# A hybrid diffusion trunk on one core: the beginning of the kernel rebuilt around un-modulated pooling

## The chip, the cores and the metric

The kernel runs on one core of one Trainium2 chip, as one program. The metric is device time in microseconds (us) of one execution; lower is better. The engines are named as in the profile: PE (TensorE, matrix products), DVE (VectorE), ACT (ScalarE), POOL (GpSimd) and SP (SyncE, which here only issues transfers). PEld is PE's loading of weights.

## The reference

The reference is one inference step of four layers over 128 context tokens and 256 latent tokens of width 1024. Each layer has a token mixer and a convolutional feed-forward block (FFN), and each of these eight sub-layers is modulated by vectors taken from a conditioning vector. What the change touches is the very first sub-layer, the pooling mixer of layer 0, and the modulation vectors that it needs:

```python
def modulation(cond, w, b):                      # six vectors of 1024 for each layer
    m = jax.nn.silu(cond) @ w + b
    return m.reshape(m.shape[:-1] + (N_MOD, D_MODEL))
def modulate_in(x, mod, k, g):
    return rms_norm(x, g) * (1.0 + mod[:, None, 3 * k + 1]) + mod[:, None, 3 * k]
def gated_residual(x, out, mod, k, g):
    return x + mod[:, None, 3 * k + 2] * rms_norm(out, g)
def pool_mixer(h, w, scale):
    ...
        mean = (csg[:, hi] - csg[:, lo]) / (hi - lo).astype(jnp.float32)[None, :, None]
        outs.append(mean - hf[..., sl])          # for each of four window lengths, 256 channels each
    p = jnp.stack(outs, axis=2).astype(h.dtype)
    y = jnp.einsum('blgc,gcd->blgd', p, w).reshape(h.shape)
    return y * scale
```

## The kernel before

All five engines run instruction lists written out by hand and meet at semaphores; each engine executes its own list strictly in order, and so does SP, which issues nearly all transfers. So a transfer that waits on SP holds back all transfers behind it.

**Pieces.** The modulation vectors are products of a two-column conditioning vector with `w_mod`. One vector of 1024 takes four pieces of 1024 KB (`MOD_PIECES = 4`); `load_mod(p)` loads piece p, `mod_piece(p)` multiplies it on PE (8 small matmuls; the trace counts 16) and then frees its buffer through the semaphore `mod_used`. Before the first FFN, 32 pieces pass: 20 for the first five vectors (SCALE0, SHIFT0, GATE0, SCALE1, SHIFT1) in seven buffers (`START_SLOTS = 7`, piece p in buffer p mod 7, so that load p waits until PE has used p-7), then 12 for the next three vectors in nine buffers. Below they are called p0 to p31. DVE's `mod_vector(i)` transposes a finished vector out of PSUM, and `coefficient` multiplies in the norm gains.

**The beginning.** PE's list (`pool_mix`) multiplies p0 to p7; turns the first scale and shift into rows, which ACT copies (`copy_row`) and stores to DRAM; SP reads them back broadcast over all partitions (`row0`, two transfers of 1024 KB). PE multiplies p8 to p11. DVE makes the modulated rows `h_rows` from x, the inverse norm and the two broadcast rows. Then PE pools: for each of eight blocks k of 128 channels, one matmul of 129 columns and two of 257 against `pool_m`, into bank 6 or 7 in turn; ACT rounds the result to `h_hi`, DVE makes the remainder `h_lo` and frees the bank (`pooled_lo`). Then p12 to p19, then the pooling mixer's weights (72 matmuls), then the gated residual of the three token chunks, between which p20 to p31 are multiplied and the three chunks are turned for the FFN (`turn_unit`). The FFN's first matmul (line 1693) needs all three turned chunks, and in PE's list the third turn stands behind p31.

**The gate.** The residual needs the gate vector GATE0 as a broadcast row: PE turns it (`turn_gate(0)`), ACT stores it, SP loads it as `gb` (`load_gate(0)`); DVE's `weigh` waits for it.

Of the kernel before, what the change touches and what calls it, by code (L numbers as in the profile page):

```python
# [14 lines left out]
P = 128  # L15
D = 1024
# [134 lines left out]
def build_trunk(nc, a, out):  # L151
# [4 lines left out]
    with ExitStack() as ctx:  # L156
# [50 lines left out]
        with ExitStack() as part:  # L207
            pool_m = sb("pool_m", [P, len(WINDOWS), POOL_W], F32, part)
            row0 = sb("row0", [P, 2, 2, D], F32, part)
            h_rows = sb("h_rows", [P, 3, D], F32, part)  # L210
            mod_more = sb("mod_more", [P, START_SLOTS - 2, 2 * D], F32, part)
# [5 lines left out]
        with ExitStack() as part:  # L217
            sb("mod_row0_under", [P, len(WINDOWS), POOL_W], F32, part)
            mod_row0 = sb("mod_row0", [P, 2, 2 * D], F32, part)
# [46 lines left out]
        rows_dram = nc.dram_tensor("rows_dram", [2 + 2 * DEPTH, 16 * P], F32, kind="Internal").ap()  # L266
# [14 lines left out]
        log_dt = flat_wk[:, 704:896]  # L281
        x_end = by_dir(flat_wk[:, 1536:2048])
# [18 lines left out]
        def mod_bank(i):  # L301
            if i < START_VECTORS:
                return bank(3 if i % 2 else 5)[:, 0:MOD_BANK_COLS]
# [25 lines left out]
        row0_loaded = sem("row0_loaded")  # L329
# [105 lines left out]
        LOADS0 = 16 * 9  # L435
# [98 lines left out]
        def _(sp):  # L534
# [19 lines left out]
            def load_gate(t):  # L554
                if t:
                    sp.wait_ge(weighed, event(t, 0))
                sp.wait_ge(row_stored[t % 2], 16 * (t // 2 + 2))
                sp.dma_start(gb[:, :, :].rearrange("p s n -> p (s n)"),
                             rows_dram[2 + t:3 + t, :].broadcast_to([P, 2 * D])).then_inc(gb_loaded, 16)
# [26 lines left out]

# [238 lines left out]
        def _(act):  # L825
# [60 lines left out]

            def transition(t, n):
# [25 lines left out]
            def ffn_in(l):  # L913
                s = lin[f"ffn_in{l}"]
                p0 = l * PAIRS
                for j in range(FFN_TILES):
# [7 lines left out]
                    if j == 3:  # L924
                        copy_row(2 + 2 * l + 1)
# [7 lines left out]
            def ssd_conv():  # L933
                s = lin["ssd_conv"]
                for j in range(CONV_TILES):
# [3 lines left out]
                    if j == 3:  # L939
                        copy_row(4)  # L940
# [68 lines left out]
            def conf_mix():  # L1009
# [17 lines left out]
                for m in range(2 * KD):  # L1027
# [10 lines left out]
                    if m == 3:  # L1038
                        copy_row(6)
# [32 lines left out]
            def qk_mix():  # L1072
                s = lin["qk"]
                for i in range(QK + 1):
                    if i < QK:
# [6 lines left out]
                        if i == 3:  # L1082
                            copy_row(8)
# [49 lines left out]
            copy_row(1)  # L1133
            round_to(2)
            copy_row(2)
            for k in range(KD):
                act.wait_ge(pooled, k + 1)
                act.activation(h_hi[:, k, :], bank(6 + k % 2)[:, 0:COLS], ACT.Copy).then_inc(pooled_hi, 1)
            transition(0, lin["ffn_in0"].n0)
# [34 lines left out]
        def _(vec):  # L1174
# [54 lines left out]
            def weigh(t, c):  # L1229
# [7 lines left out]
                if t in (0, 4):  # L1237
                    if t == 4:
# [1018 lines left out]
```

## Time and profile before

| | us |
|---|---|
| median of 3 runs (2098.22 to 2098.79) | 2098.58 |
| the profiled execution, its own time | 2101.43 |
| its span in the trace | 2099.7 |
| first matmul of the first FFN in the trace | 128.39 |
| PE busy in the span | 1970.1 (94%) |

The profiled execution took 2.85 us more than the median, of which 1.73 us lie outside its span. The busy share is one over the whole span; the beginning, which is the only part that the change edits, looks quite different and is read from its own rows.

### The profile page before, as it was taken

The page shows a single profiled execution, that of the slowest core. Times are in us where ns is not written, and L with a number is a line of the kernel's source. Part 1 is how long each engine was busy: PE and PEld are TensorE (multiplying, and loading weights), DVE is VectorE, ACT ScalarE, POOL GpSimd, SP SyncE. Part 2 cuts the span into 40 slices and gives each one's busy share as a digit, 9 for nine tenths or more (in the row PEclk, how much of TensorE's full clock was granted, in tenths as well). Part 3 has the DMA queues.
Part 4 walks back from the last instruction along what each step waited for, and adds up shares of the span by engine and source line. Part 5 has one row for each costly group of instructions (what it writes and reads, how often), then busy time and mean ns, then how long its engine had stood idle before and what let it go on. Part 6 is the DMA issues. An engine that isn't in the chain of part 4 may idle for free.

```text
span 2099.7 us, 30072 instructions
## 1 busy us (share of the span) xinstructions
PE 1970.1 (94%) x11801; PEld 1744.9 (83%) x11801; DVE 1195.5 (57%) x1773; ACT 919.6 (44%) x1552; POOL 701.1 (33%) x515
## 2 busy tenths in 40 slices
PE   3779999999999989999999998899999969899998
PEld 1469998799998877799987865799987857799986
DVE  0567772366534565777733853777723674777722
ACT  1244442444545554544423424544424434544422
POOL 0033324233334445332243741323242321332342
PEclk6889999999999999999999999999999979999999
DMA  9954346544330135543454674444364413244442
GB/s 366 372 222 150 122 120 220 179 134 130 116 126 20 34 121 224 213 148 121 127 205 171 223 196 180 182 145 127 121 215 179 180 46 111 77 144 122 129 123 78
DMA packets 80667, 326.41 MB, mean 155 GB/s; under 512 B 9072, under 2 KB 17808, under 8 KB 66704
## 3 DMA queue, kind: packets, MB, share of 16 engines
q1 hardware_dynamic: 78928, 322.57, 44.5%
q8 instruction: 94, 1.54, 0.3%
q10 hardware_dynamic: 1600, 1.93, 0.3%
q14 instruction: 45, 0.37, 0.1%
HBM read 319.34 MB, written 5.12 MB: 155 GB/s over the span
## 4 chain that ended last, share of the span: by engine, by line
PE 82%; DVE 6%; ACT 4%; DMA 3%; issue 2%; POOL 1%; SPq 1%; DVEq 0%; ACTq 0%; POOLq 0%
PE pair L1693 17%; PE pair L1695 17%; PE pair L1694 17%; PE pair L1727 7%; PE pair L1728 6%; PE pair L1729 6%; PE pair L1841 3%; DMA mod_more<-in_w_mod 2%; DVE x L1253 2%; PE pair L1935 1%; ACT junk L863 1%; PE pair L1881 1%; PE pair L1846 1%; DMA ssd_cols<-in_ssd_cols 1%; DVE wk L1244 1%
## 5 line engine op out<-in xcount | busy, mean ns | idle before, releaser
L712 POOL TENSOR_TENSOR w_lo<-raw,w_hi 128x512 fp32r<-128x512 f32 (+1 forms) x375 | 574.7, 1534 | 1150.9 <-ACT w_hi L835 1150.7
L1693 PE MATMUL pair<-h_hi,w_hi 128*128 128x386 f32 (+1 forms) x2008 | 689.4, 343 | 18.8 <-POOL h_lo L719 16.2
L1695 PE MATMUL pair<-h_hi,w_lo 128*128 128x386 f32 (+1 forms) x2008 | 684.7, 341 | 0.0
L1694 PE MATMUL pair<-h_lo,w_hi 128*128 128x386 f32 (+1 forms) x2008 | 683.9, 341 | 0.0
L1186 DVE TENSOR_TENSOR w_lo<-raw,w_hi 128x512 fp32r<-128x512 f32 x351 | 430.6, 1230 | 317.1 <-ACT w_hi L835 317.0
L835 ACT ACTIVATE w_hi<-raw 128x1024 fp32r<-128x1024 f32 x375 | 392.8, 1050 | 285.3 <-PE pair L1729 224.5
L1693 PEld LDWEIGHTS pair<-h_hi,w_hi 128*128 128x128 f32 (+1 forms) x2008 | 381.8, 190 | 24.4 <-POOL h_lo L719 22.1
L1694 PEld LDWEIGHTS pair<-h_lo,w_hi 128*128 128x128 f32 (+1 forms) x2008 | 382.6, 191 | 0.9
L1695 PEld LDWEIGHTS pair<-h_hi,w_lo 128*128 128x128 f32 (+1 forms) x2008 | 381.7, 190 | 0.3
L1310 DVE SCALAR_TENSOR_TENSOR acc<-pair,taps,acc 128x385 f32<-128x385 f32 x176 | 108.8, 618 | 214.8 <-ACT acc L922 214.8
L922 ACT ACTIVATE acc<-pair,taps 128x386 f32<-128x386 f32 x176 | 117.4, 667 | 238.3 <-PE pair L1695 238.3
L1728 PE MATMUL pair<-w_hi,g 128*128 128x512 f32 x528 | 208.5, 395 | 0.0
L1729 PE MATMUL pair<-w_lo,g 128*128 128x512 f32 x528 | 208.4, 395 | 0.0
L1727 PE MATMUL pair<-w_hi,g 128*128 128x512 f32 x528 | 208.3, 395 | 0.0
L1727 PEld LDWEIGHTS pair<-w_hi,g 128*128 128x128 f32 x528 | 99.2, 188 | 23.4
L1728 PEld LDWEIGHTS pair<-w_hi,g 128*128 128x128 f32 x528 | 99.3, 188 | 23.3
L1729 PEld LDWEIGHTS pair<-w_lo,g 128*128 128x128 f32 x528 | 99.2, 188 | 23.3
L920 ACT ACTIVATE g<-gate 128x386 fp32r<-128x386 f32 x84 | 44.3, 527 | 162.4 <-DVE gate L1323 162.4
L1317 DVE SCALAR_TENSOR_TENSOR acc<-pair,taps,acc 128x385 f32<-128x385 f32 x176 | 108.5, 616 | 3.2
L991 ACT ACTIVATE mod_raw<-pair,shift 128x128 f32<-128x128 f32 x192 | 53.8, 375 | 32.0 <-PE pair L1846 31.9
L719 POOL TENSOR_TENSOR h_lo<-stage,h_hi 128x512 fp32r<-128x512 f32 x21 | 32.0, 1522 | 92.4 <-ACT h_hi L885 92.4
L1448 DVE TENSOR_TENSOR mod_raw<-mod_raw,pair 128x512 f32<-128x512 f32 x48 | 32.3, 685 | 53.3 <-ACT mod_raw L991 53.3
(277 smaller groups left out, 2195.6 us busy)
## 6 DMA issues: line engine op xcount, KB each, us to landing
raw<-in_ffn_in SPq DMA_DIRECT2D x176, 512.0 KB, 3.5
raw<-in_ffn_out SPq DMA_DIRECT2D x88, 512.0 KB, 3.6
mod_raw<-in_w_mod SPq DMA_DIRECT2D x32, 1024.0 KB, 7.5
mod_base<-in_w_mod SPq DMA_DIRECT2D x31, 1024.0 KB, 7.4
mod_more<-in_w_mod SPq DMA_DIRECT2D x20, 1024.0 KB, 13.7
raw<-in_ssd_conv SPq DMA_DIRECT2D x32, 512.0 KB, 3.5
gb<-rows_dram SPq DMA_DIRECT2D x8, 1024.0 KB, 5.2
raw<-in_ssd_z SPq DMA_DIRECT2D x16, 512.0 KB, 3.4
```

The source lines that it names most:

```text
L712: pool.tensor_tensor(w_lo[:, m % SLOTS, 0:w], raw[:, m % SLOTS, 0:w], w_hi[:, m % SLOTS, 0:w].bitcast(F32), ALU.subtract).then_inc(w_low_p ...
L835: act.activation(w_hi[:, m % SLOTS, 0:w], raw[:, m % SLOTS, 0:w], ACT.Copy).then_inc(w_rounded, 1)
L922: act.activation(acc[:, j % 4, :], tile_bank(j)[:, 0:COLS], ACT.Identity, scale=taps[:, l, j, 1:2], bias=taps[:, l, j, 3:4]).then_inc(acc_ ...
L1186: vec.tensor_tensor(w_lo[:, m % SLOTS, w0:w1], raw[:, m % SLOTS, w0:w1], w_hi[:, m % SLOTS, w0:w1].bitcast(F32), ALU.subtract).then_inc(w_ ...
L1310: vec.scalar_tensor_tensor(out=acc[:, j % 4, 1:COLS], in0=b[:, 0:COLS - 1], scalar=taps[:, l, j, 0:1], in1=acc[:, j % 4, 1:COLS], op0=ALU. ...
L1317: vec.scalar_tensor_tensor(out=acc[:, j % 4, 0:COLS - 1], in0=b[:, 1:COLS], scalar=taps[:, l, j, 2:3], in1=acc[:, j % 4, 0:COLS - 1], op0= ...
L1693: ten.matmul(to, wh, h_hi[:, k, cols], start=k == 0, stop=False, skip_group_check=True)
L1694: ten.matmul(to, wh, h_lo[:, k, cols], start=False, stop=False, skip_group_check=True)
L1695: ins = ten.matmul(to, wl, h_hi[:, k, cols], start=False, stop=k == KD - 1, skip_group_check=True)
L1727: ten.matmul(to, hi[:, k, cols], wh, start=first, stop=False)
L1728: ten.matmul(to, lo[:, k, cols], wh, start=False, stop=False)
L1729: ins = ten.matmul(to, hi[:, k, cols], wl, start=False, stop=last)
```

## The change

Before, the rows were normalized, scaled and shifted (by broadcast rows) and then pooled. Now the rows are only normalized and then pooled; since pooling is linear along tokens and the scale and shift are per channel, the scale is applied to the pooled block by ACT (`pooled_scaled`) and the shift, times the column sums of the pool matrix, is added by DVE (`pooled_shifted`). The column sums come from 12 matmuls of `pool_m` with a matrix of ones. The two rows through DRAM are gone. PE's own loop over the eight blocks is unchanged, and with it its wait, from block k = 2 on, for the remainder of block k-2 (`pooled_lo`, k-1). The order of transfers, of the pieces on PE, and of the work in the first transition is new.

```diff
@@ SP: order of transfers
-            for p in range(START_SLOTS):
+            for p in range(MOD_PIECES):
                 load_mod(p)
...
+            for p in range(MOD_PIECES, START_SLOTS):
+                load_mod(p)
             sp.dma_start(pool_m[:, :, :], a["pool_m"]).then_inc(loaded0, 16)
...
+            load_mod(START_SLOTS)
+            load_to(2)
+            for p in range(START_SLOTS + 1, 3 * MOD_PIECES):
                 load_mod(p)
-            for r in range(2):
-                sp.wait_ge(row_stored[r], 16)
-                sp.dma_start(row0[:, r, :, :].rearrange("p s n -> p (s n)"),
-                             rows_dram[r:r + 1, :].broadcast_to([P, 2 * D])).then_inc(row0_loaded, 16)
-            for p in range(10, 16):
+            sp.dma_start(rowc[:, :], a["pool_scale"].broadcast_to([P, D])).then_inc(pool_scale_loaded, 16)
+            for p in range(3 * MOD_PIECES, 3 * MOD_PIECES + START_SLOTS):
                 load_mod(p)
-            load_to(2)
             load_gate(0)
-            for p in range(16, MOD_PIECES * START_VECTORS):
+            for p in range(3 * MOD_PIECES + START_SLOTS, MOD_PIECES * START_VECTORS):
                 load_mod(p)
             load_to(4)
+            for to, name in ((taps, "taps"), (ssd_taps, "ssd_taps"), (dt_rows, "dt_rows"), (ssd_cols, "ssd_cols")):
+                sp.dma_start(to[tuple(slice(None) for _ in to.shape)], a[name]).then_inc(tables_loaded, 16)
@@ ACT: scale, then round
+            for k in range(KD + 1):
+                if k < KD:
+                    act.wait_ge(pooled, k + 1)
+                    if k >= 2:
+                        act.wait_ge(pooled_lo, k - 1)
+                    for s, cols in enumerate((slice(0, LAT0), slice(LAT0, COLS))):
+                        ins = act.activation(pooled_v[k % 2][:, cols], bank(6 + k % 2)[:, cols], ACT.Identity,
+                                             scale=coef[:, 0, 0, s, k:k + 1])
+                    ins.then_inc(pooled_scaled, 1)
+                if k:
+                    act.wait_ge(pooled_shifted, k)
+                    act.activation(h_hi[:, k - 1, :], pooled_v[(k - 1) % 2], ACT.Copy).then_inc(pooled_hi, 1)
@@ DVE: shift, then remainder
+            for k in range(KD + 1):
+                if k < KD:
+                    vec.wait_ge(pooled_scaled, k + 1)
+                    v = pooled_v[k % 2]
+                    for s, cols in enumerate((slice(0, LAT0), slice(LAT0, COLS))):
+                        ins = vec.scalar_tensor_tensor(out=v[:, cols], in0=pool_sums[:, k // 2, cols],
+                                                       scalar=modc[:, 0, SHIFT0, s, k:k + 1], in1=v[:, cols],
+                                                       op0=ALU.mult, op1=ALU.add)
...
+                if k:
+                    vec.wait_ge(pooled_hi, k)
+                    vec.tensor_tensor(h_lo[:, k - 1, :], pooled_v[(k - 1) % 2], h_hi[:, k - 1, :].bitcast(F32),
+                                      ALU.subtract).then_inc(pooled_lo, 1)
@@ PE: pool_mix
-                for p in range(2 * MOD_PIECES):
+                for p in range(MOD_PIECES):
                     mod_piece(p)
...
+                ten.wait_ge(loaded0, LOADS0)
+                for g in range(len(WINDOWS)):
+                    to = bank((0, 1, 2, 4)[g])
+                    ten.matmul(to[:, 0:LAT0], ones[:, :], pool_m[:, g, 0:LAT0], start=True, stop=True, skip_group_check=True)
...
-                for p in range(3 * MOD_PIECES, START_VECTORS * MOD_PIECES):
+                for p in range(2 * MOD_PIECES, 3 * MOD_PIECES):
                     mod_piece(p)
+                turn_gate(0)
...
-                fill(0, 0, 3)
+                ten.wait_ge(weighed, event(0, 0) + 1)
+                for p in range(3 * MOD_PIECES, 4 * MOD_PIECES):
+                    mod_piece(p)
                 turn_unit(0, 0)
-                fill(0, 3, 7)
+                for p in range(4 * MOD_PIECES, START_VECTORS * MOD_PIECES):
+                    mod_piece(p)
+                ten.wait_ge(mod_read, START_VECTORS)
+                fill(0, 0, 7)
                 turn_unit(0, 1)
                 fill(0, 7, None)
                 turn_unit(0, 2)
```

SP's list, from the transfers behind `pool_m` to the first FFN weights. `mod_raw` and `mod_more` are pieces, `raw` weights, `rowc` the pooling scale, `gb` the gate row; the brackets name the semaphores that an issue waits for. Before:

```order
L542 DMA mod_raw<-in_w_mod 128x2048 [waits mod_used] x2
L542 DMA mod_more<-in_w_mod 128x2048 [waits mod_used]
L577 DMA row<-rows_dram 128x2048 [waits row_stored0]
L577 DMA row<-rows_dram 128x2048 [waits row_stored1]
L542 DMA mod_more<-in_w_mod 128x2048 [waits mod_used] x4
L542 DMA mod_raw<-in_w_mod 128x2048 [waits mod_used] x2
L551 DMA raw<-in_pool 128x1024 x2
L558 DMA gb<-rows_dram 128x2048 [waits row_stored0]
L542 DMA mod_more<-in_w_mod 128x2048 [waits mod_used] x4
L551 DMA raw<-in_ffn_in 128x1024 x2
```

Now:

```order
L545 DMA mod_raw<-in_w_mod 128x2048 [waits mod_used]
L554 DMA raw<-in_pool 128x1024 x2
L545 DMA mod_raw<-in_w_mod 128x2048 [waits mod_used]
L545 DMA mod_more<-in_w_mod 128x2048 [waits mod_used] x3
L577 DMA rowc<-in_pool_scale 128x1024
L545 DMA mod_more<-in_w_mod 128x2048 [waits mod_used] x2
L545 DMA mod_raw<-in_w_mod 128x2048 [waits mod_used] x2
L545 DMA mod_more<-in_w_mod 128x2048 [waits mod_used] x3
L561 DMA gb<-rows_dram 128x2048 [waits row_stored0]
L545 DMA mod_more<-in_w_mod 128x2048 [waits mod_used]
L554 DMA raw<-in_ffn_in 128x1024 x2
```

The two row transfers are gone, and the gate row moved from behind p15 to behind p18.

PE's list around the pooling loop, of which the first and the last block stand here. Lines 1664 and 1711 are the pieces (8 matmuls each), 2093 to 2097 and 2131 to 2148 products with `pool_m`, 2116 and 2169 the first of the mixer's weights. Before:

```order
L1664 MATMUL pair<-mod_raw,cond 32x256 x8
L1664 MATMUL pair<-mod_more,cond 32x256 x24
L1672 MATMUL pair<-ident,coef 16x128
L2093 MATMUL pair<-pool_m,h_rows 128x129
L2097 MATMUL pair<-pool_m,h_rows 128x257 x2
...
L1664 MATMUL pair<-mod_more,cond 32x256 x16
L1664 MATMUL pair<-mod_raw,cond 32x256 x16
L1664 MATMUL pair<-mod_more,cond 32x256 x32
L2116 MATMUL pair<-w_hi,h_hi 128x256
```

Now:

```order
L2131 MATMUL pair<-pool_m,ones 128x129
L2134 MATMUL pair<-pool_m,ones 128x257 x2
L1711 MATMUL pair<-mod_more,cond 32x256 x24
L1711 MATMUL pair<-mod_raw,cond 32x256 x8
L2144 MATMUL pair<-pool_m,h_rows 128x129
L2148 MATMUL pair<-pool_m,h_rows 128x257 x2
...
L1711 MATMUL pair<-mod_raw,cond 32x256 x8
L1711 MATMUL pair<-mod_more,cond 32x256 x24
L1719 MATMUL pair<-ident,coef 16x128
L2169 MATMUL pair<-w_hi,h_hi 128x256
```

The sums and p4 to p7 now stand ahead of the loop, p8 to p11 moved from ahead of it to behind it, and p12 to p19 left this stretch for one further down, behind the mixer's weights.

DVE's list in the pooling loop, from its second block on. Before, `L1618 TENSOR_TENSOR h_lo<-pair,h_hi` stood eight times in a row; now:

```order
L1656 SCALAR_TENSOR_TENSOR stage<-wk,modc,stage 128x129 [waits pooled_scaled]
L1656 SCALAR_TENSOR_TENSOR stage<-wk,modc,stage 128x257
L1665 TENSOR_TENSOR h_lo<-stage,h_hi 128x386 [waits pooled_hi]
L1656 SCALAR_TENSOR_TENSOR stage<-wk,modc,stage 128x129 [waits pooled_scaled]
L1656 SCALAR_TENSOR_TENSOR stage<-wk,modc,stage 128x257
L1665 TENSOR_TENSOR h_lo<-stage,h_hi 128x386 [waits pooled_hi]
```

The remainder of block k now stands behind the shift of block k+1.

## Rows read from the trace of the kernel before

**Rows 1.** Page: chain that ended last, share of the span by engine.

```profile
PE 82%; DVE 6%; ACT 4%; DMA 3%; issue 2%; POOL 1%; SPq 1%; DVEq 0%; ACTq 0%; POOLq 0%
```

**Rows 2.** Chain that ended last, 0 to 220 us: start us, us, what.

```profile
96.67 23.20 DMA mod_more<-in_w_mod
119.92 1.93 PE pair L1664 x16
128.39 0.66 PE pair L1693
```

**Rows 3.** Timeline, 0 to 40 us: start, us, operation, [idle <-releaser].

```profile
6.26 1.94 PE L1664 MATMUL pair<-mod_raw,cond 128*32 128x256 f32 x16 [6.26 <-DMA mod_raw<-in_w_mod]
21.10 1.94 PE L1664 MATMUL pair<-mod_more,cond 128*32 128x256 f32 x16 [0.55 <-DMA mod_more<-in_w_mod]
32.89 1.06 ACT L1130 ACTIVATE junk<-x 128x1024 bf16<-128x1024 f32 x1 [30.04 <-DMA ssd_cols<-in_ssd_cols]
```

**Rows 4.** Stretches: engines' busy time (x instructions), PEclk, DMA share, GB/s.

```profile
37.00:42.00 5.00, 3.73 (x38) 1.56 (x34) 1.03 (x5) 1.78 (x6) 0.00 (x0) 0.50 0.35 107
63.00:69.00 6.00, 5.99 (x17) 4.59 (x18) 2.88 (x4) 3.25 (x5) 3.45 (x2) 0.53 0.29 95
77.00:83.00 6.00, 4.95 (x92) 2.50 (x80) 0.80 (x3) 0.00 (x0) 0.00 (x0) 1.00 0.84 313
```

**Rows 5.** SP's own waits, 0 to 135 us: total us, times, longest.

```profile
SPq L558 <- DMA rows_dram<-grow: 22.2, 1, 22.2
```

**Rows 6.** Timeline of the pooling loop, 62 to 78 us.

```profile
62.84 0.80 PE L2093 MATMUL pair<-pool_m,h_rows 128*128 128x129 f32 x2 [6.98 <-DVE h_rows L1614]
63.43 1.92 PE L2097 MATMUL pair<-pool_m,h_rows 128*128 128x257 f32 x4
65.14 0.64 PE L2093 MATMUL pair<-pool_m,h_rows 128*128 128x129 f32 x2
70.60 0.49 PE L2093 MATMUL pair<-pool_m,h_rows 128*128 128x129 f32 x2
70.93 1.03 PE L2097 MATMUL pair<-pool_m,h_rows 128*128 128x257 f32 x4
72.00 0.49 ACT L1138 ACTIVATE h_hi<-pair 128x386 fp32r<-128x386 f32 x1 [0.95 <-PE pair L2097]
72.52 0.56 DVE L1618 TENSOR_TENSOR h_lo<-pair,h_hi 128x386 fp32r<-128x386 f32 x1 [0.88 <-ACT h_hi L1138]
73.14 0.49 PE L2093 MATMUL pair<-pool_m,h_rows 128*128 128x129 f32 x2
75.52 1.93 PE L1664 MATMUL pair<-mod_more,cond 128*32 128x256 f32 x32
```

**Rows 7.** Timeline of the first transition, 110 to 114 us.

```profile
111.46 1.36 DVE L1271 TENSOR_SCALAR stage<-pair,coef,modc 128x128 f32<-128x128 f32 x4
112.35 1.49 ACT L876 ACTIVATE stage<-pair,modc,coef 128x128 f32<-128x128 f32 x4
```

**Rows 8.** Groups by line and shape, whole run: busy us, mean ns.

```profile
L922 ACT ACTIVATE acc<-pair,taps 128x386 f32<-128x386 f32 x176 | 117.4, 667 | 238.3 <-PE pair L1695 238.3
L1310 DVE SCALAR_TENSOR_TENSOR acc<-pair,taps,acc 128x385 f32<-128x385 f32 x176 | 108.8, 618 | 214.8 <-ACT acc L922 214.8
```

**Rows 9.** DMA issues, 0 to 135 us: KB each, us from issue to landing.

```profile
gb<-rows_dram SPq DMA_DIRECT2D x1, 1024.0 KB, 4.5
```

**Rows 10.** Timeline of the first gated residual, 86 to 92 us.

```profile
88.26 1.22 DVE L1240 TENSOR_TENSOR wk<-pair,rowc 128x1024 f32<-128x1024 f32 x1 [2.35 <-PE pair L2118]
90.77 1.23 DVE L1244 TENSOR_TENSOR wk<-wk,gb 128x1024 f32<-128x1024 f32 x1 [1.29 <-ACT junk L847]
```

**Rows 11.** Stretches around two changes of the granted clock (columns as rows 4).

```profile
68.00:69.00 1.00, 1.00 (x5) 0.88 (x5) 0.56 (x1) 0.02 (x1) 0.11 (x1) 0.66 0.75 164
97.00:102.00 5.00, 2.70 (x38) 1.22 (x36) 3.68 (x5) 3.86 (x9) 1.27 (x1) 1.00 1.01 419
102.00:103.00 1.00, 0.59 (x12) 0.39 (x16) 1.00 (x4) 1.00 (x2) 0.00 (x0) 0.91 1.06 442
```

More of the change, by code:

```diff
@@ L281, in build_trunk @@
         log_dt = flat_wk[:, 704:896]
+        pool_sums = flat_wk[:, 0:len(WINDOWS) * COLS].rearrange("p (g n) -> p g n", g=len(WINDOWS))
+        pooled_v = [flat_stage[:, k * 512:k * 512 + COLS] for k in range(2)]
         x_end = by_dir(flat_wk[:, 1536:2048])
@@ L302, in mod_bank @@
             if i < START_VECTORS:
[L303 removed]
+                return bank((5, 3, 5, 0, 1)[i])[:, 0:MOD_BANK_COLS]
             r = (i - START_VECTORS) % END_VECTORS
@@ L885, in unit_high, with transition0 @@
                 act.activation(h_hi[:, :, cols], stage[:, e % 2, :, :], ACT.Copy).then_inc(h_hi_ready, 1)
+            def transition0(n):
+                for c in range(3):
+                    first(0, c)
+                    second(0, c)
+                round_to(n + 2)
+                for c in range(3):
+                    unit_stage(0, c)
+                    unit_high(0, c)
+                act.wait_ge(tables_loaded, 64)
+                round_to(n + 4)
             def transition(t, n):
@@ L1131, in _ @@
                 root(c)
-            copy_row(0)
[L1133 to L1139, printed above, removed]
+            act.wait_ge(coef_ready, 1)
+            for k in range(KD + 1):
[10 more added lines that the diff above has]
+                    act.activation(h_hi[:, k - 1, :], pooled_v[(k - 1) % 2], ACT.Copy).then_inc(pooled_hi, 1)
+            round_to(2)
+            copy_row(0)
+            transition0(lin["ffn_in0"].n0)
             for l in range(DEPTH):
@@ L1280, in unit_low, with transition0 @@
                                   ALU.subtract).then_inc(h_lo_dve, 1)
+            def transition0(n):
+                for c in range(2):
+                    weigh(0, c)
+                    residual(0, c)
+                    unit(0, c)
+                mod_vector(3)
+                coefficient(0, 2)
+                weigh(0, 2)
+                residual(0, 2)
+                low_to(n + 2)
+                mod_vector(4)
+                vec.wait_ge(mod_done, START_VECTORS)
+                unit_stage(0, 0)
+                unit(0, 2)
+                unit_low(0, 0)
+                for c in (1, 2):
+                    unit_stage(0, c)
+                    unit_low(0, c)
+                vec.wait_ge(tables_loaded, 64)
+                low_to(n + 4)
+                end_vectors(0)
             def transition(t, n):
@@ L1601, in _ @@
             vec.wait_ge(consts, CONSTS)
+            for c in range(3):
+                invert(c)
+                vec.tensor_scalar(h_rows[:, c, :], x[:, c, :], inv[:, c:c + 1], None, ALU.mult).then_inc(rows_ready, 1)
+            vec.wait_ge(sums_made, 1)
+            for g in range(len(WINDOWS)):
+                ch.did(vec.tensor_copy(pool_sums[:, g, :], bank((0, 1, 2, 4)[g])[:, 0:COLS]))
             mod_vector(0)
@@ L2078, in pool_mix @@
             def pool_mix():
-                for p in range(2 * MOD_PIECES):
+                for p in range(MOD_PIECES):
                     mod_piece(p)
-                ten.wait_ge(coef_ready, 1)
-                turn_row(0, coef[:, 0, 0, :, :].rearrange("p s k -> p (s k)"))
-                ten.wait_ge(mod_done, 2)
-                turn_row(1, modc[:, 0, SHIFT0, :, :].rearrange("p s k -> p (s k)"))
-                for p in range(2 * MOD_PIECES, 3 * MOD_PIECES):
+                ten.wait_ge(loaded0, LOADS0)
+                for g in range(len(WINDOWS)):
+                    to = bank((0, 1, 2, 4)[g])
+                    ten.matmul(to[:, 0:LAT0], ones[:, :], pool_m[:, g, 0:LAT0], start=True, stop=True, skip_group_check=True)
+                    for c in (1, 2):
+                        at = LAT0 + (c - 1) * (LAT + 1)
+                        ins = ten.matmul(to[:, LAT0:COLS], ones[:, :], pool_m[:, g, at:at + LAT + 1],
+                                         start=c == 1, stop=c == 2, skip_group_check=True)
+                ins.then_inc(sums_made, 1)
+                for p in range(MOD_PIECES, 2 * MOD_PIECES):
                     mod_piece(p)
-                turn_gate(0)
                 ten.wait_ge(rows_ready, 3)
```

74 lines of the change are left out of this document (29 added, 45 removed).

## The prediction

> **What bounds the kernel now.** The page comes first: PE is busy 94% of the span (table above) and makes 82% of the chain that ended last [rows 1]. Behind the first FFN matmul the program is the same row for row, and PE is its bound; so the change is worth what it does to the moment of that matmul, 128.39 us. The chain up to there, read next, ends in one load: p31, issued at 96.67, is used by PE at 119.92, and 8.5 us of turning and rounding lie between that and 128.39 [rows 2]. The beginning therefore waits for bytes, and the question is how long the DMA engines need for all that lies up to p31.
>
> The stretches show when they work. In a busy stretch seven pieces start on PE between 6.26 and 21.10, so 1024 KB take 14.84 / 6 = 2.47 us [rows 3]; I call 1024 KB a unit. There are three holes: DMA share 0.35 from 37 to 42, 0.29 from 63 to 69, 0.84 from 77 to 83, idle 3.25 + 4.25 + 1 = 8.5 us [rows 4]. The middle one is a wait on SP: the gate row's issue waited 22.2 us for its stored row [rows 5], what was queued ran out, and nothing behind it could start. The ledger up to p31: 32 pieces, x 1.5 units, `pool_m` 1.26, pooling weights 1, four FFN chunks 2, gate row 1, two `row0` rows 2, scale 0.5, tables and gains 0.65: 41.9 units, 103.5 us; a start of 6.26 - 2.47 = 3.8; about 2 us for six small transfers (from p6 at 21.10 to the first use at 32.89 pass 3.9 units, 9.6 us, in 11.8 [rows 3]); holes 8.5. Sum 117.8, against 119.92.
>
> **The change, as the same ledger.** The two `row0` rows go: 2 units, 4.9 us saved. All else is loaded still. So the change stands or falls by the holes, and a hole opens when SP stands at a piece whose buffer PE has not freed. Two such places are new.
>
> *First hole.* p15 takes the buffer of p8, and p8 now stands behind PE's whole pooling loop. When does that loop end?
> - SP's start: p0 to p3, x, gains, p4 to p6, `pool_m`: 13.65 us for p3, then 5.9 units (14.6) and 0.7 for two small transfers: everything for the rows is there at 28.95, against 32.89 before [rows 3].
> - 12 sum matmuls are four blocks of the pooling loop's shapes. [...] So two blocks at 2.30, one at 1.9, one at 1.36: 36.8. DVE normalizes the rows (three passes) meanwhile, and its four copies of the sums and first two vectors lie beside PE's p4 to p7.
> - p4 to p7: 4 x 0.95 (two pieces in 1.93 [rows 6]): 40.6.
> - Blocks 0 and 1: 2 x 1.36 (70.60 to 71.96 [rows 6]): 43.3.
> - From then on the loop is one chain. PE's block k+1 waits for the remainder of block k-1; on DVE that stands behind the shift of block k; which waits for ACT's scale of block k; which waits for PE's block k. Before, the same wait hung on one round of ACT 0.49 and DVE 0.56 in two banks, PE going on in the other [rows 6]; eight blocks took 62.84 to 75.52, 12.7 us.
> - The pair of ACTIVATEs (129 and 257 columns): no such row exists. Four of 128 columns take 1.49, so the next starts after 0.37 [rows 7]; 386 columns take 0.67 [rows 8]; between them 257 columns are about 0.56. Pair 0.93; no less than one of 386, 0.67. The pair of shifts on DVE likewise from 1.36 / 4 = 0.34 less the overlap, 0.32 [rows 7], and 0.62 for 385 columns [rows 8]: 0.32 + 0.51 = 0.83, at least 0.62. The remainder 0.56, handovers 0.04, 0.03 and 0.06 [rows 6].
> - Length of one round: at the high clock 1.36 + 0.93 + 0.83 + 0.56 + 0.13 = 3.81 us; at the low clock, where a block takes 62.84 to 65.35, 2.51 [rows 6], 4.96.
> - Which clock? PE would work 1.36 of 3.81 us, a share of 0.36. The nearest rows: from 97 to 102 PE worked 2.70 of 5 us at the high clock, and within 102 to 103 the clock fell [rows 11]. So it should fall in the loop as well, after some us: I take block 2 high, 3 to 7 low. First remainder: 43.3 + 0.04 + 0.93 + 0.03 + 0.83 + 0.56 = 45.7; one high round 49.5; four low rounds 69.35; block 7 2.57 later, 71.9; p8 1.93 (low clock, as in [rows 3]), 73.85.
> - A lone transfer of one unit lands 4.5 us after its issue [rows 9]: p15 at 78.45.
>
> Meanwhile the queue is empty: behind `pool_m` come p7 to p14, pooling weights and scale, 9.5 units, done at 28.95 + 23.5 = 52.4 (p11 waits for p4's use, at 37.8, in time). The hole is 78.45 - 2.47 - 52.4 = 23.6 us.
>
> *Second hole.* p16 to p18 and the gate row follow without a gap, 88.35 (its row is stored at about 82: p11 used at 79, then vector, turn, copy and store). p19, next on SP, takes the buffer of p12; PE's p12 now waits for the first weighing, which waits for the gate row. Weighing took 88.26 to 92.0 [rows 10], 3.75; p12 another 1.0; issue to landing 4.6: p19 at 97.7, where 2.47 would do. Hole 6.9 us. SP's queue behind p19 waits with it: FFN chunks, tables, p20 to p31.
>
> *Rest.* From p19: two FFN chunks 1 unit, tables 0.5 unit and 1.4 us for four small transfers, p20 to p28, two chunks, p29 to p31: 14.5 units and 1.4, 37.2 us. p31 at 134.9, 15.0 us later than 119.92. The reordered residuals are costed at nothing, since this DMA time covers them: DVE's three weighings and what now stands between them take some 23 us from 92 on, so PE's new wait for the fifth vector ends at about 115; p20 to p31 (12 x 0.95), one turn and the unchanged 8.5 us make 136. Were the loads sooner, that chain would end the beginning, 7 us below the 134.9 + 8.5 = 143.4 of the loads.
>
> Sum: minus 4.9 for bytes, plus 30.5 of new holes, minus 8.5 of old holes, minus the 2.1 by which the ledger falls short of 119.92: plus 15. On the profiled execution 2101.43 + 15.0 = 2116.4; that execution lies 2.85 above the median shown, so against the median 2098.58 the forecast is **2113.5 us**.
>
> [...]
>
> **Rivals.**
> 1. *The clock stays high through the loop*: five low rounds and block 7 fall to high ones. First remainder 45.7, five rounds of 3.81, block 7, p8 0.97: 67.15, 6.7 earlier: plus 8.3. With the shortest pairs (0.67, 0.62) a round is 3.34, 2.4 less: plus 5.9. For it: from 97 to 102 the clock held for 5 us of half-busy work; against it: it fell right after [rows 11], the loop is less busy than that, and it lasts longer.
> [...]
> 2. *The clock never rises before the loop*: sums 9.4, pieces 7.7, blocks 4.8, all rounds 4.96: p8 at 82.55, 8.7 later: plus 23.7. Against it: dense work from 62.84 raised it within 68 to 69 [rows 6, 11], and sums and pieces are as dense.
> 3. *The loop overlaps as before*, its stages running side by side: 12.7 us from 40.6, p8 at 54.3, 19.6 earlier: minus 4.7, 2094 us. It decides from p8 at 58.9 on, a round of 2.2 us; the three engines' shortest rows in series make 3.34, and the waits make them a series.
> 4. *No change*: holes as large as those removed, p8 at 55 to 63. It needs rounds of 1.5 to 3.0 us; between rivals 1 and 3.
>
> **How the numbers follow.** About 0.2% (4.2 us) is what a measurement of this kernel can tell from none. Forecast (mostly low rounds) 0.47, rival 1 0.27, rival 2 0.14, rival 3 0.05, rival 4 0.07. The range leaves out rivals 3 and 4 and the far end of 2: plus 5.5 to plus 22, 2104 to 2120.5. Slower 0.88, same 0.07, faster 0.05; the first three cases are all slower.
>
> **What would show it.** Right: DMA share near zero from about 53 to 75 and again for 7 us after the gate row's landing; PE's blocks in the pooling loop 3.8 to 5 us apart, each released by DVE's remainder; p15 released on SP by p8; the first FFN matmul near 143. Wrong: blocks under 2.3 us apart, or p15 issued before 55, would put it at 128 or earlier; a first FFN matmul that does not follow p31 by about 8.5 us would mean that another chain has taken over.

## The result, and the profile after

The change made the kernel slower: 2118.25 us (median of 5 runs, 2114.94 to 2118.53) against 2098.79 us (median of 5 runs, 2098.22 to 2105.13), a ratio of 1.0083, 95% interval 1.0071 to 1.0094. The ratio is taken over the runs of the set; the two medians alone would give 1.0093. The forecast was 2113.5 us in 2104 to 2120.5. The profiled execution took 2116.63 us with a span of 2114.9, 15.2 us more than that of before.

The page gives the chain that ended last, share of the span by engine, as [rows 1]:

```profile
PE 82%; DVE 7%; ACT 5%; issue 2%; DMA 2%; POOL 1%; SPq 0%; DVEq 0%; ACTq 0%; POOLq 0%
```

It still names PE first, and nothing in it points at the beginning. The chain up to the first FFN matmul, which answers to [rows 2], says where the time is (start us, us, what):

```profile
75.17 4.79 DMA rows_dram<-grow
79.97 7.18 DMA gb<-rows_dram
113.56 5.03 PE pair L1711 x48
118.61 16.66 DMA mod_more<-in_w_mod
135.32 1.94 PE pair L1711 x16
143.71 0.66 PE pair L1740
```

p31 is used at 135.32 instead of 119.92, and the first FFN matmul starts at 143.71 instead of 128.39: 15.3 us, all of the difference between the two profiled executions. Behind it 1971.2 us pass up to the end of the span; before, 1971.3.

SP's list shows the two places where it stood (start us, us; the first row holds p14, issued at once, and p15, which waited; the last is p19):

```profile
38.94 30.98 SPq L545 DMA_DIRECT2D mod_raw<-in_w_mod  x2
70.89 2.06 SPq L545 DMA_DIRECT2D mod_more<-in_w_mod  x3
79.97 0.33 SPq L561 DMA_DIRECT2D gb<-rows_dram  x1
93.02 0.33 SPq L545 DMA_DIRECT2D mod_more<-in_w_mod  x1
```

The stretches show the holes that this leaves (columns as [rows 4]; the third from the right is the granted clock, the next the DMA share):

```profile
45.00:50.00 5.00, 2.51 (x6) 1.61 (x6) 1.22 (x3) 1.55 (x6) 0.00 (x0) 0.64 1.02 428
50.00:52.00 2.00, 0.62 (x3) 0.62 (x4) 1.22 (x3) 0.48 (x2) 0.00 (x0) 0.50 0.57 242
52.00:70.00 18.00, 11.76 (x47) 6.97 (x50) 5.06 (x13) 5.33 (x14) 0.00 (x0) 0.50 0.01 2
70.00:73.00 3.00, 2.54 (x44) 1.15 (x36) 2.36 (x3) 1.68 (x2) 2.19 (x2) 0.96 0.80 259
73.00:84.00 11.00, 8.96 (x73) 8.65 (x73) 1.44 (x4) 0.27 (x1) 1.27 (x1) 1.00 0.96 378
84.00:86.00 2.00, 0.00 (x0) 0.00 (x0) 0.00 (x0) 0.00 (x0) 0.00 (x0) 1.00 0.39 156
86.00:93.50 7.50, 2.48 (x24) 1.19 (x28) 3.81 (x4) 2.55 (x5) 0.00 (x0) 0.59 0.02 4
93.50:95.00 1.50, 1.50 (x28) 0.80 (x24) 1.06 (x3) 0.34 (x2) 0.00 (x0) 0.79 0.76 87
95.00:135.00 40.00, 21.28 (x280) 10.32 (x272) 16.60 (x29) 12.81 (x24) 6.37 (x4) 0.75 1.01 420
```

Idle share by length: 0.9 + 17.8 + 0.6 = 19.3 us in the first hole, 1.2 + 7.4 + 0.4 = 9.0 us in the second, 28.3 us in all where before had 8.5. From 95 to 135 the engines never ran dry (DMA share 1.01).

The pooling loop, which answers to [rows 6], one round at the high clock and one at the low (granted clock 1.00 from 40 to 46, 0.50 from 47 to 70; timeline):

```profile
43.34 0.49 PE L2144 MATMUL pair<-pool_m,h_rows 128*128 128x129 f32 x2 [2.08 <-DVE h_lo L1665]
46.78 0.80 PE L2144 MATMUL pair<-pool_m,h_rows 128*128 128x129 f32 x2 [2.08 <-DVE h_lo L1665]
47.38 1.92 PE L2148 MATMUL pair<-pool_m,h_rows 128*128 128x257 f32 x4
49.34 0.73 ACT L1148 ACTIVATE stage<-pair,coef 128x129 f32<-128x129 f32 x2 [3.45 <-PE pair L2148]
50.10 0.75 DVE L1656 SCALAR_TENSOR_TENSOR stage<-wk,modc,stage 128x129 f32<-128x129 f32 x2 [3.37 <-ACT stage L1148]
50.77 0.55 DVE L1665 TENSOR_TENSOR h_lo<-stage,h_hi 128x386 fp32r<-128x386 f32 x1
51.38 0.80 PE L2144 MATMUL pair<-pool_m,h_rows 128*128 128x129 f32 x2 [2.08 <-DVE h_lo L1665]
```

These are four stages of three engines in a row, with only ACT's rounding beside them: PE 2.56, ACT 0.76, DVE's shift 0.67 and its remainder 0.61 make the 4.60 us from 46.78 to 51.38. In each round PE waits 2.08 us for DVE's remainder.

### The profile page after: what moved, and what is told of

Its sections match the earlier page's. It is cut to its first block, busy times and chain, and to the rows that moved or that the text cites. A ratio compares the mean times of both kernels' runs of the same rounds, so it can differ in the third digit from the quotient of the medians.

```text
span 2114.9 us, 30146 instructions
## 1 busy us (share of the span) xinstructions
PE 1974.4 (93%) x11823; PEld 1750.6 (83%) x11823; DVE 1197.0 (57%) x1790; ACT 924.8 (44%) x1566; POOL 701.9 (33%) x515
## 4 chain that ended last, share of the span: by engine, by line
PE 82%; DVE 7%; ACT 5%; issue 2%; DMA 2%; POOL 1%; SPq 0%; DVEq 0%; ACTq 0%; POOLq 0%
PE pair L1740 17%; PE pair L1742 17%; PE pair L1741 17%; PE pair L1774 6%; PE pair L1775 6%; PE pair L1776 6%; PE pair L1888 3%; DVE x L1269 2%; PE pair L1982 1%; ACT junk L861 1%; DMA pool_m<-in_pool_m 1%; DVE wk L1260 1%; PE pair L1928 1%; PE pair L1893 1%; DVE w_lo L1203 1%
## 5 line engine op out<-in xcount | busy, mean ns | idle before, releaser
L1774 PEld LDWEIGHTS pair<-w_hi,g 128*128 128x128 f32 x528 | 99.2, 188 | 23.4
L1776 PEld LDWEIGHTS pair<-w_lo,g 128*128 128x128 f32 x528 | 99.2, 188 | 23.4
```

What stands on the lines that cost most here:

```text
L1774: ten.matmul(to, hi[:, k, cols], wh, start=first, stop=False)
L1776: ins = ten.matmul(to, hi[:, k, cols], wl, start=False, stop=last)
```

## The experiments

Three theories were written down before the runs. **H** is the prediction's: what counts is the DMA time lost while SP stands at a transfer that must wait. **B**: the whole cost lies in p15 standing behind p8. **C**: what grew is the serial chain of pooling, gate row and residuals; loads are late only because nobody needs them sooner. Line numbers in the experiments' rows differ by up to some 30 from those above.

The kernel before was run again beside each set, and each ratio is to the runs of its own set (medians 2100.34 us beside runs 1 to 4, 2099.26 beside 5 to 7, 2098.34 beside 8). The last column is the idle time of the DMA engines from 4 us to p31's use, added up over steps of 1 us.

| kernel | median us (runs) | ratio to before, 95% interval | p15 issued | p19 issued | p31 on PE | first FFN matmul | DMA idle up to p31 |
|---|---|---|---|---|---|---|---|
| before | 2098.79 (5) | 1 | 43.8 | 76.7 | 119.92 | 128.39 | 10.6 |
| changed | 2118.25 (5) | 1.0083 (1.0071 to 1.0094) | 69.6 | 93.0 | 135.32 | 143.71 | 30.3 |
| 1: p8 ahead | 2119.04 (4) | 1.0091 (1.0076 to 1.0107) | 39.5 | 93.7 | 135.93 | 142.82 | 32.2 |
| 2: first hole filled | 2109.13 (4) | 1.0049 (1.003 to 1.0068) | 69.2 | 92.8 | 128.52 | 135.41 | 23.4 |
| 3: second hole filled | 2105.90 (6) | 1.0032 (1.002 to 1.0045) | 70.8 | 94.6 | 128.99 | 135.88 | 23.4 |
| 4: bank wait | 2099.38 (10) | 0.9995 (0.9986 to 1.0004) | 52.0 | 74.4 | 116.62 | 125.11 | 12.9 |
| 5: runs 3 and 4 together | 2090.44 (6) | 0.9952 (0.994 to 0.9964) | 53.5 | 76.2 | 111.96 | 118.85 | 7.9 |
| 6: pieces between blocks | 2091.98 (6) | 0.9957 (0.9943 to 0.9972) | 44.0 | 64.3 | 108.48 | 117.12 | 4.8 |
| 7: busier PE | 2107.97 (6) | 1.0035 (1.0023 to 1.0047) | 62.0 | 82.8 | 124.83 | 131.7 | 20.6 |
| 8: run 6, gate row later | 2087.53 (5) | 0.9942 (0.9929 to 0.9956) | 44.2 | 54.4 | 103.97 | 110.87 | 1.7 |

Taking the last column from p31's time leaves 102.3 to 105.6 us in the changed kernel and all eight runs, and 109.3 before, which loads two rows (4.9 us) more. So the idle time accounts for the differences in p31 to within some 3 us.

### Run 1: p8 to p11 back ahead of the pooling loop

```diff
-                for p in range(MOD_PIECES, 2 * MOD_PIECES):
+                for p in range(MOD_PIECES, 3 * MOD_PIECES):
                     mod_piece(p)
...
-                for p in range(2 * MOD_PIECES, 3 * MOD_PIECES):
-                    mod_piece(p)
                 turn_gate(0)
```

> The changed kernel with one step undone: PE multiplies p8 to p11 ahead of the pooling loop again, so that p15 finds its buffer free. Theory H (holes: the delay is DMA time lost while SP stands at a waiting transfer): the first hole does not close but moves behind p18, where SP stands at the gate row, whose vector is still turned behind the loop, and the loop itself starts some 6 us later because p11 lands at about 43.6; first FFN matmul at about 140 (143.7 in the changed kernel, 128.4 before), total some 4 us under the changed kernel. Rival B (p15 behind p8 is the whole cost): 19 us under it, first FFN matmul at 125. Rival C (the serial chain of pooling and residuals is what counts, and the loads are late only because nobody needs them): no gain, or 2 us slower, since the loop starts later.

No gain. p15 to p18 were issued by 46, and then SP stood at the gate row instead (timeline of SP, and stretches):

```profile
40.64 5.29 SPq L545 DMA_DIRECT2D mod_more<-in_w_mod  x3
83.37 0.33 SPq L561 DMA_DIRECT2D gb<-rows_dram  x1
93.73 0.33 SPq L545 DMA_DIRECT2D mod_more<-in_w_mod  x1
```
```profile
61.00:83.00 22.00, 9.33 (x26) 6.52 (x27) 8.85 (x18) 6.87 (x15) 3.43 (x2) 0.50 0.01 4
```

The hole moved from 52 to 70 to 61 to 83, and p19 was issued at 93.7 as before. B falls: p8's place alone is worth nothing, since the next transfer in SP's list waits for the same loop. H had expected 4 us of gain, with the later start of the loop counted in. What came instead: the loop ended 6.7 us later (its last block starts at 71.82 instead of 65.16), the gate row's store and load took 6.0 us less on an idle queue (1.43 and 4.54 us instead of 4.79 and 7.18), and so the gate row landed 0.8 us later. No gain is what C had said; this run alone does not tell H from C.

### Runs 2 and 3: the same bytes into the first or into the second hole

The FFN chunks 2 and 3, the tables, p27 and p28 leave their places behind p19; no engine's work is touched. Run 2 issues them ahead of p15, run 3 ahead of p19. The edit of run 3, on SP:

```diff
             load_gate(0)
-            for p in range(3 * MOD_PIECES + START_SLOTS, MOD_PIECES * START_VECTORS):
-                load_mod(p)
             load_to(4)
             for to, name in ((taps, "taps"), (ssd_taps, "ssd_taps"), (dt_rows, "dt_rows"), (ssd_cols, "ssd_cols")):
                 sp.dma_start(to[tuple(slice(None) for _ in to.shape)], a[name]).then_inc(tables_loaded, 16)
+            for p in (27, 28):
+                load_mod(p)
+            for p in range(3 * MOD_PIECES + START_SLOTS, MOD_PIECES * START_VECTORS):
+                load_mod(p)
...
-            load_ends(0, *range(MOD_SLOTS))
+            load_ends(0, *range(MOD_SLOTS - 2))
```

Run 2: 

> The changed kernel with SP's order alone edited: the two FFN chunks, the four tables and p27 and p28 (4 units of 1024 KB less a little, none of which waits for anything) are issued ahead of p15, so that they move while SP would stand there. No engine's work changes. Theory H: these bytes (about 10 us with their small transfers) leave the stretch behind p19; p31 lands at about 124 to 125 instead of 135.3, first FFN matmul at 133 to 134, total 10 us under the changed kernel. Rival C: first FFN matmul stays at 143 to 144, no change.

Run 3: 

> The same bytes as in the run before it, issued between the gate row and p19 instead, to move while SP stands at p19 (the DMA engines were idle from 84.5 to 94 in the changed kernel). Theory H: that hole is filled to the brim, p19 lands 1 to 2 us later than now, p31 9 us sooner; first FFN matmul at 134 to 135.5, total 8 to 9.5 us under the changed kernel. Rival C: no change.

The first FFN matmul came 8.3 and 7.8 us sooner, p31 6.8 and 6.3 sooner; the rest is that p31 and the last turn ran at the high clock (p31 1.07 us instead of 1.94; granted clock over the two 1.00 in both runs, 0.57 in the changed kernel). The gate row and the residuals came no sooner: PE's wait for the fifth vector ended at 113.34 in run 2 and 115.11 in run 3, 113.56 in the changed kernel (chain, run 2 and run 3):

```profile
113.34 4.92 PE pair L1715 x48
115.11 5.16 PE pair L1713 x48
```

C allowed no change; it falls, and H stands: DMA time put into a hole comes back at the end. Not all of it came back (3.5 units and the small transfers are 8.6 + 1.4 us). In run 2 the second hole was 1.1 us longer, and SP now also stood at p20, whose buffer p13 leaves only after the weighing (SP's list below); in run 3 p15 was issued 1.2 us later, and the first hole was 1.5 us longer. Some 2 us in each are not accounted for.

```profile
92.79 0.33 SPq L545 DMA_DIRECT2D mod_more<-in_w_mod  x1
95.07 1.19 SPq L545 DMA_DIRECT2D mod_raw<-in_w_mod  x2
```

### Run 4: PE waits for the bank, not for the remainder

ACT's scale is the only reader of the PSUM bank now; the wait for DVE's remainder was left over from before. One line on PE:

```diff
                     if k >= 2:
-                        ten.wait_ge(pooled_lo, k - 1)
+                        ten.wait_ge(pooled_scaled, k - 1)
```

> The changed kernel with one wait on PE changed: from the third pooling block on PE waits for ACT's scale of the block two before (which is what frees the PSUM bank now) instead of for DVE's remainder. Nothing else. Theory H with the loop as its cause: PE leaves the round, a round is ACT's scale 0.76, DVE's shift 0.67 and remainder 0.56 and a handover, about 2.05 us, or PE's block of 2.3 us at the low clock; the loop ends at 52 to 55 instead of 67.6, p15 is issued at 54 to 57 instead of 69.6, and all behind it moves up: first FFN matmul at 127 to 129, total 15 to 17 us under the changed kernel, about level with the kernel before. If the clock alone made the rounds long (they stay 4.6 us whatever PE waits for): no change.

Measured 125.1, 18.6 us sooner; the kernel is level with before. PE, ACT and DVE now work side by side (timeline):

```profile
45.39 0.49 PE L2144 MATMUL pair<-pool_m,h_rows 128*128 128x129 f32 x2 [0.72 <-ACT stage L1148]
45.72 1.03 PE L2148 MATMUL pair<-pool_m,h_rows 128*128 128x257 f32 x4
46.69 0.74 ACT L1148 ACTIVATE stage<-pair,coef 128x129 f32<-128x129 f32 x2 [0.93 <-DVE h_lo L1665]
47.45 0.75 DVE L1656 SCALAR_TENSOR_TENSOR stage<-wk,modc,stage 128x129 f32<-128x129 f32 x2 [0.86 <-ACT stage L1148]
47.47 0.49 PE L2144 MATMUL pair<-pool_m,h_rows 128*128 128x129 f32 x2 [0.73 <-ACT stage L1148]
```

A round is 2.08 us (45.39 to 47.47); it is DVE's and ACT's now (0.76, 0.67 and 0.65 from ACT's start through DVE's two stages to ACT's next), PE waits 0.72 in it, and the granted clock stays at 1.00 from 40 to 55. p15 is issued at 52.0, so the first hole is down to some 2.4 us. What is left is the second, some 8.3 us: SP stood at p19 from 65.6 to 74.4.

### Run 5: the second hole filled as well

Runs 3 and 4 put together, no other edit.

> The changed kernel with two edits that were each run alone: PE's loop waits for ACT's scale (as in the run of the bank wait) and the FFN chunks, the tables, p27 and p28 are issued between the gate row and p19 (as in the run of the second hole). H (time is lost while SP stands at a waiting transfer): the first hole is gone with the bank wait, what is left is the second, from about 67 to 74.5 in the run of the bank wait; 3.5 units and the tables (about 8.6 us of DMA time) fill it, so p31 moves from 116.6 to about 109.5 and the first FFN matmul from 125.1 to 117.5 to 119; about 2092 us, ratio to before 0.9965. C (the serial chain of residuals sets the end once the loop is repaired): PE's wait for the fifth vector ended at 95.9 in the run of the bank wait, p20 to p31 and the last turn are over 13 us behind it, and with 8.5 us that makes 118 as well if pieces are there; so C's floor is about the same and forbids more than about 7 us. If the end stays at 125, both are wrong.

Measured 118.85 and 2090.44 us: faster than both kernels, and where H and C had both put it, so the time alone does not tell them apart. Its chain turns from engines to a load at 102.69:

```profile
97.28 5.39 PE pair L1713 x48
102.69 9.23 DMA mod_more<-in_w_mod
111.96 1.07 PE pair L1713 x16
```

p31 takes the buffer of p22, which PE reaches only when the fifth vector has been read, at 97.28. That looks like a part for C, but the stretches do not show one: the engines were idle earlier, and hardly behind 80 (0.97 up to 112, with the last 2 us at 0.41, where p31 is the last to land). So p31's late issue cost nothing that these rows show; what is left lies at p15's issue (53.5) and at the gate row's (66.3):

```profile
52.00:56.00 4.00, 4.00 (x67) 2.04 (x65) 2.28 (x7) 2.29 (x6) 0.00 (x0) 1.00 0.40 100
66.00:70.00 4.00, 4.00 (x36) 4.00 (x36) 0.00 (x0) 0.00 (x0) 0.00 (x0) 1.00 0.72 256
80.00:112.00 32.00, 18.24 (x264) 9.92 (x263) 15.61 (x28) 12.54 (x24) 5.63 (x4) 0.79 0.97 402
```

### Run 6: no transfer waits for the residuals

To run 4 this adds: p8 to p11 one after each of the pooling blocks 2 to 5, p12 to p19 ahead of the mixer's products (vector four back in bank 3, five in bank 5), and the residuals in the order of before on PE, ACT and DVE. The core of it on PE:

```diff
                     ins.then_inc(pooled, 1)
-                for p in range(2 * MOD_PIECES, 3 * MOD_PIECES):
+                    if 2 <= k < 2 + MOD_PIECES:
+                        mod_piece(2 * MOD_PIECES + k - 2)
+                for p in (12, 13):
                     mod_piece(p)
                 turn_gate(0)
+                for p in range(14, START_VECTORS * MOD_PIECES):
+                    mod_piece(p)
```

> The bank wait on ACT's scale, PE multiplies p8 to p11 between the pooling blocks 2 to 5, p12 to p19 stand ahead of the mixer's products again (vectors four and five in banks 3 and 5 as in the kernel before), and the residuals have the order of the kernel before. Nothing on SP should stand at a buffer or at the gate row any more. H: from 28.7 on the queue carries 30 units up to p31 without a hole, 74 us and 1.4 us for small transfers, so p31 at about 104.5 and the first FFN matmul at 113 to 116; 2087 to 2090 us, ratio 0.995. C: weighing starts only behind p19 and the products, at about 77, and the three residuals take 23 us and the turns and pieces 13 more, so the first FFN matmul at 119 or later, 2092 or more.

The first FFN matmul came at 117.1, between what H (113 to 116) and C (119 or later) had said, and in time the run is not to be told from run 5. Its SP list and stretches name the rest:

```profile
46.26 4.91 SPq L545 DMA_DIRECT2D mod_more<-in_w_mod  x3
63.92 0.33 SPq L561 DMA_DIRECT2D gb<-rows_dram  x1
```
```profile
58.00:64.00 6.00, 5.24 (x49) 2.47 (x53) 3.79 (x6) 0.53 (x2) 2.44 (x2) 0.50 0.54 221
64.00:66.00 2.00, 2.00 (x36) 0.98 (x28) 0.00 (x0) 0.00 (x0) 0.00 (x0) 0.82 0.58 233
```

These are 2.8 + 0.8 = 3.6 us idle while SP stood at the gate row, about as much as p31 came behind the 104.5 of H: the kind of hole that run 1 had shown, only shorter.

### Run 7: what the low clock cost

Two further matmuls of 386 columns, used by nothing, in each round of the changed kernel's loop:

```diff
                     if k >= 2:
+                        if k == 2:
+                            ten.wait_ge(mod_read, 2)
+                        for _ in range(2):
+                            ten.matmul(bank(0)[:, 0:COLS], ones[:, :], pool_m[:, 0, 0:COLS], start=True, stop=True,
+                                       skip_group_check=True)
                         ten.wait_ge(pooled_lo, k - 1)
```

> The changed kernel with two further matmuls of 386 columns (their result is used by nothing) ahead of PE's wait in each round of the pooling loop from block 2 on, about 1.6 us at the high clock, which lie in PE's wait of 2.1 us. This asks what the low clock in the loop cost. If the clock stays high (the further work makes PE busy about 0.85 of a round), rounds stay at 3.44 instead of 4.59: five rounds, block 7 and p8 to p11 come 5.8 to 8 us sooner, p15 is issued at about 62 to 64 instead of 69.6, and by H the first FFN matmul comes 6 to 7 us sooner, at 137, about 2111 us: PE doing more work makes the kernel faster. If the clock falls all the same, a round becomes 4.6 to 5.6 us and the kernel 0 to 6 us slower than the changed one. C gives no change or slower in both cases.

More work on PE made the kernel faster: ratio 1.0035 against 1.0083. The rounds stay at 3.44 us (stretch and timeline):

```profile
48.00:62.00 14.00, 10.86 (x58) 6.55 (x60) 5.10 (x13) 4.82 (x13) 0.00 (x0) 1.00 0.22 92
```
```profile
42.41 0.49 PE L2149 MATMUL pair<-pool_m,h_rows 128*128 128x129 f32 x2 [0.79 <-DVE h_lo L1665]
45.85 0.49 PE L2149 MATMUL pair<-pool_m,h_rows 128*128 128x129 f32 x2 [0.79 <-DVE h_lo L1665]
```

p15 was issued 7.6 us sooner, as expected, but the first FFN matmul came 12.0 us sooner, not 6 to 7. The gate row landed in 4.60 us instead of 7.18 (chain):

```profile
73.10 4.60 DMA gb<-rows_dram
```

That makes the weighing 9.4 us sooner (77.79 against 87.23) and p19 10.3; and p31 and the last turn ran at the high clock (1.07 and 1.04 us, granted clock 1.00), another 1.5. The size of the clock's cost was underrated, its sign was right.

### Run 8: the gate row behind what need not wait

```diff
-            for p in range(3 * MOD_PIECES, 3 * MOD_PIECES + START_SLOTS):
-                load_mod(p)
-            load_gate(0)
-            for p in range(3 * MOD_PIECES + START_SLOTS, MOD_PIECES * START_VECTORS):
+            for p in range(3 * MOD_PIECES, MOD_PIECES * START_VECTORS):
                 load_mod(p)
...
+            for p in (27, 28):
+                load_mod(p)
+            load_gate(0)
...
-            load_ends(0, *range(MOD_SLOTS))
+            load_ends(0, *range(MOD_SLOTS - 2))
```

> The kernel of the run with p8 to p11 between the pooling blocks, with one edit on SP: p19, the two FFN chunks, the tables, p27 and p28 are issued ahead of the gate row instead of behind it. In that run SP stood at the gate row until 63.9 while what was queued ran out: DMA share 0.54 from 58 to 64 and 0.58 from 64 to 66, 3.6 us idle. H (time is lost while SP stands at a waiting transfer): the idle time goes, p31 is used at about 104.5 to 105 instead of 108.5 and the first FFN matmul comes at 113 to 114 instead of 117.1; 2 to 4 us below the kernel without the edit, about 2087 us. C (the residual chain sets the end): weighing starts some 2 us sooner only if the products do (p19 lands sooner); the last turn stood at 110.3 right behind p31 there, and DVE was done with the third unit at 102, so C's floor is about 104 plus 7: it allows 1 to 6 us and does not tell apart; if the first FFN matmul stays at 117, H's account of that hole is wrong. A gate row that now lands behind 8.5 units, at about 77, must not be later than the weighing needs it (79.2 there).

The hole is gone, and p31 is used at 103.97 (stretches, and PE's timeline):

```profile
58.00:64.00 6.00, 5.04 (x69) 2.51 (x73) 4.00 (x6) 0.74 (x2) 2.64 (x2) 0.72 1.01 421
66.00:104.00 38.00, 24.96 (x284) 15.82 (x272) 20.52 (x31) 14.80 (x30) 2.75 (x3) 0.91 1.00 414
```
```profile
103.97 1.07 PE L1685 MATMUL pair<-mod_more,cond 128*32 128x256 f32 x16 [1.40 <-DMA mod_more<-in_w_mod]
```

110.87 is below the 113 to 114 expected because p31 came 0.5 to 1 us sooner than expected, and because p31 and the last turn ran at the high clock (1.07 and 1.04 us at a granted clock of 1.00, in run 6 1.93 and 1.92 at 0.50). It is also where C had put its floor (104 plus 7), so this run does not tell H from C by its time; PE still waited 1.40 us for p31's load, so the load came last, by little. This is the changed kernel's idea with one wait and the orders on SP, PE, ACT and DVE put right: 2087.53 us, ratio 0.9942, the lowest of all, though its interval overlaps those of runs 5 and 6. Its first FFN matmul is 8.0 us ahead of run 5's, its profiled span only 3.4 us shorter; where the rest went is in the last section.

## Why the prediction was right, step by step

**The ledger held.** Without the two row transfers the prediction's terms give 39.9 units x 2.47 + 3.8 + 2 = 104.4 us for p31 in a beginning without holes; run 8, which has none, reached 103.97. In the other kernels the rest is holes, to within the 3 us that the last column of the table leaves.

**First hole: right in place and cause, too large by 4.3 us.** p15 was released by p8, p8 stood behind the loop, each block was released by DVE's remainder, and blocks 2 and 3 to 7 ran at the high and the low clock as the forecast case had it (granted clock 0.64 from 45 to 50, 0.50 from 50 to 70). What was mis-sized: everything up to blocks 0 and 1 ended at 41.3, not 43.3, since the clock rose sooner than assumed and the sums ended at 35.3, not 36.8 (PE began them at 28.70, the granted clock was 0.50 up to 32, 0.65 from 32 to 33 and 1.00 from 33 on); and the low round was 4.60, not 4.96. Of the 2.30, 2.30, 1.9 and 1.36 us for the four blocks of the sums, 1.9 was the author's estimate, which no row of before shows; in the changed kernel these blocks took 2.31, 1.93, 1.09 and 1.19 us from start to start (28.70, 31.01, 32.94, 34.03, 35.22). In the round it was the pairs, for which the rows gave no form: ACT's took 0.73, not 0.93, DVE's 0.67 up to the remainder, not 0.83. So p15 was issued at 69.6 instead of 73.85. Two smaller misses about cancel: the queue ran dry at 51.2 instead of 52.4, and the engines were busy again about 0.8 us after p15's issue, where the prediction counted 2.1.

**Second hole: right in place and cause, too small by 2.1 us.** The gate row landed at 87.15 (predicted 88.35) and p19 was issued at 93.02 (predicted about 93.1). That the latter fits so well is luck: the gate row came 1.2 us sooner, and p12, which PE began at 91.02, took the 2 us of the low clock and not 1.0 (granted clock 0.50 from 91 to 93). The hole began earlier than predicted: the gate row's bytes had all flowed by about 85, two us before it landed (DMA share 0.39 from 84 to 86, 0.02 after), and the prediction counted the hole from the landing.

**Rest.** The holes sum to 28.3 instead of 30.5, yet p31 came at 135.32, 0.4 later than predicted, so 2.6 us are missing from its sum. The ledger of before had fallen short by much the same, 2.1 us; in both traces the steps of 1 us show 2 us of short dips outside the named holes (30.3 against 28.3, 10.6 against 8.5). Another part may be the rate: from 70 to 84 the queue was busy for 13.0 us and moved 3 x 259 + 11 x 378 = 4935 KB, for which the 424 GB/s of the stretch from 40 to 45 need 11.6. The prediction had no such term; in that stretch the gate row was stored and read back. That p31 came within 0.4 us is thus in part luck: minus 4.3 + 2.1 + 2.6. PE's wait for the fifth vector ended at 113.56 (about 115 predicted), covered by the loads as costed; the 8.5 us from p31 to the first FFN matmul were 8.4.

**Rivals.** Rival 1 (clock high) is what run 7 made happen on purpose (granted clock 1.00 from 48 to 62); the prediction gave it plus 8.3, and the trace of run 7 puts the first FFN matmul 3.3 us behind that of before. So the clock costs more than the five rounds: behind them the gate row took 4.60 us instead of 7.18, and p31 and the last turn 1.5 us less. Rival 2 (clock never high) did not come: the granted clock was 1.00 from 40 to 45. In the changed kernel's loop it fell once, between 46 and 47 (0.68 in that microsecond), and stayed at 0.50 until 70. Rival 3 (a loop that overlaps) is run 4 in its mechanism: a round of 2.08, p15 at 52. The prediction had minus 4.7 for it, the trace gives minus 3.3, and the timing (0.9986 to 1.0004) cannot tell it from no change. It did not happen by itself because of one stale wait.

**The time.** The profiled executions differ by 15.2 us where 15.0 was forecast. The timed medians differ by 19.5; 15.2 us would be a ratio of 1.0072, just inside the interval. The prediction took before's profiled execution to lie 2.85 us above its median and carried that over; after's lies 1.6 below its own, so that step failed by 4.5 us. Why single executions differ so stays open.

## What to carry to other kernels

In a stretch that is bound by loads, write the bytes up as a ledger and count only idle queue time; a transfer that must wait belongs in the queue behind everything that need not (the first FFN matmul came 7.8 us sooner in run 3 than in the changed kernel, 6.3 sooner in run 5 than in run 4, 6.2 sooner in run 8 than in run 6), and moving one waiting transfer is worth nothing while the next in the list waits for the same loop (run 1, ratio 1.0091 against 1.0083). When a new reader takes a buffer over, move the wait that frees it: the whole loss of this change hung on one semaphore (run 4, the first FFN matmul 18.6 us sooner).

## What the runs showed that was not expected

- The gate row's 8 KB store took 1.4 us in before and in run 1, where no piece was under way (DMA share 0.04 from 66 to 67 in before, 0.02 from 81.9 to 83.4 in run 1), and 4.2 to 5.3 us in the others, where 1024 KB pieces were under way when it was issued (4.79 in the changed kernel, DMA share 0.99 from 75.2 to 80). It lies on the chain to the gate row.
- Filler matmuls in a waiting loop kept the granted clock at 1.00 (run 7, 48 to 62; 0.50 from 50 to 70 in the changed kernel) and made the kernel faster (ratio 1.0035 against 1.0083).
- Behind the first FFN matmul all these kernels are the same, and the prediction took what follows as equal. The profiled executions took 1970.4 to 1972.2 us from there to the end of the span in six kernels, but 1974.9 to 1975.1 in runs 1, 6, 7 and 8, whose times are worse by some 3 us than their first FFN matmul lets expect. The loss is there when layer 2's convolution starts, and part of it already at the end of layer 1's scan. In these four the granted clock was 0.83 from 640 to 660 us behind the first FFN matmul, in the changed kernel and runs 2 to 5 it was 1.00. But before had 0.83 there too, without the loss, so the clock alone is not the cause, which stays open. It is as large as many differences that were to be told apart; that is why the first FFN matmul stands in the table.
